# Last block of a small transformer: experts multiplied densely from streamed tables, in place of gathered rows

## What is computed

```python
q = einsum('cd,de->ce', xc, w_q).reshape(C, 8, 2, 128)
s = einsum('chpk,pnk->chpn', q, sub_keys)            # 8 heads, 2 halves, 128 keys each
sv, si = top_k(s, 16)
cand = sv[:, :, 0, :, None] + sv[:, :, 1, None, :]   # 16 x 16 sums
top_v, top_pos = top_k(cand, 16)
eid = take_along_axis(cand_id, top_pos)              # si0 * 128 + si1: one of 16384 experts
gate = softmax(top_v)
act = gelu(einsum('cd,chkd->chk', xc, expert_u[eid]))
y = einsum('chk,chkd->cd', gate * act, expert_v[eid])
```

## Time and profile before

| | us |
|---|---|
| runs before | 1394.95, 1395.61, 1398.93 (median 1395.61) |
| span of the profiled execution | 1393.4 |
| TensorE busy | 1274.3 (91%) |
| VectorE busy | 813.1 (58%) |
| ScalarE busy | 436.1 (31%) |
| POOL busy | 653.1 (47%) |
| bytes moved by DMA | 406.77 MB |

### The profile page before, as it was taken

The page is one execution under the profiler, slowest core; times in us unless marked ns, Lnnn a source line. Parts: engine busy times, 40 slices in busy tenths (PEclk is TensorE's granted clock), DMA queues, the critical chain, the costliest instruction groups (busy, mean ns, idle before and its releaser), DMA issues.

```text
span 1393.4 us, 17185 instructions
## 1 busy us (share of the span) xinstructions
PE 1274.3 (91%) x6328; PEld 785.6 (56%) x6328; DVE 813.1 (58%) x1694; ACT 436.1 (31%) x1065; POOL 653.1 (47%) x647
## 2 busy tenths in 40 slices
PE   9999999999999999999999999989677887877886
PEld 8887686648886686549655565633232333323332
DVE  1776377441666387352357764879888654444445
ACT  1533344111334334212334433243323232222223
POOL 0556667431636667422104444455533645554540
PEclk9999999999999999999999999999998989998999
DMA  9544335546444344635449999999999999999995
GB/s 374 213 167 173 131 125 209 210 157 222 152 170 179 122 167 170 254 137 208 172 171 412 420 406 421 419 419 421 422 421 421 421 423 421 422 421 422 422 421 240
DMA packets 54061, 406.77 MB, mean 292 GB/s; under 512 B 6213, under 2 KB 8666, under 8 KB 11610
## 3 DMA queue, kind: packets, MB, share of 16 engines
q0 software_dynamic: 37184, 268.45, 46.5%
q1 hardware_dynamic: 15706, 136.18, 25.3%
q10 hardware_dynamic: 1088, 1.05, 0.3%
HBM read 403.53 MB, written 1.07 MB: 290 GB/s over the span
## 4 chain that ended last, share of the span: by engine, by line
PE 33%; DMA 24%; DVE 6%; ACT 3%; issue 1%; POOL 0%; DVEq 0%; ACTq 0%
DMA ring<-in_peer_uv,vM 12%; PE bank L1173 11%; PE pj L739 6%; PE pj L775 6%; DMA qM<-in_peer_uv,vM 5%; DMA xT<-in_peer_uv,vM 4%; PE pj L1036 3%; PE pj L754 3%; DMA more_rows<-in_peer_uv,vM 2%; DMA b<-in_peer_uv,vM 2%; DVE ring L1993 1%; ACT rope L1409 1%; PE bank L699 1%; DVE qM L1993 0%; PE bank L1046 0%
## 5 line engine op out<-in xcount | busy, mean ns | idle before, releaser
L739 PE MATMUL pj<-xT,ring 128*128 128x256 f32 (+1 forms) x1568 | 318.4, 363 | 0.9 <-ACT hv L1343 0.4
L739 PEld LDWEIGHTS pj<-xT,ring 128*128 128x128 f32 x1568 | 276.6, 190 | 36.5 <-issue 2.6
L674 POOL DMA_INDIRECT ring<-in_peer_uv,vM x108 | 129.8, 1202 | 124.1 <-PE bank L1173 108.2
L635 POOL TENSOR_SCALAR more_rows<-more_rows,lbt 128x256 f32<-128x256 f32 x168 | 175.7, 1046 | 16.4
L1993 DVE SCALAR_TENSOR_TENSOR ring<-ring,memT 128x1024 f32<-128x1024 f32 x110 | 133.6, 1224 | 83.9 <-DMA ring<-in_peer_uv,vM 83.2
L1407 ACT ACTIVATE rope<-vM 128x1 f32<-128x1 f32 (+2 forms) x112 | 22.6, 202 | 385.1 <-DVE ring L1993 166.1
L1173 PE MATMUL bank<-ring,causal 128*128 128x512 f32 x256 | 123.5, 629 | 20.2 <-ACT causal L1415 20.2
L775 PE MATMUL pj<-ring,yT 128*128 128x512 f32 x320 | 140.8, 594 | 0.0
L633 POOL TENSOR_SCALAR mod_part<-more_rows,lbt 128x256 f32<-128x256 f32 x24 | 22.8, 951 | 245.7 <-issue 121.3
L636 POOL TENSOR_TENSOR mod_part<-mod_part,more_rows 128x256 f32<-128x256 f32 x168 | 128.4, 765 | 14.0
L1173 PE MATMUL bank<-ring,tri 128*128 128x512 f32 x176 | 84.8, 624 | 18.5 <-ACT tri L1415 18.4
(11 more groups left out here) (386 smaller groups left out, 2053.0 us busy)
## 6 DMA issues: line engine op xcount, KB each, us to landing
ring<-in_units SPq DMA_DIRECT2D x43, 2048.0 KB, 9.5
more_rows<-in_w_ada SPq DMA_DIRECT2D x24, 1024.0 KB, 4.9
ring<-in_units SPq DMA_DIRECT2D x2, 1536.0 KB, 8.0
ring<-in_peer_uv,vM POOLq DMA_INDIRECT x108, 21.4
memT<-in_mem SPq DMA_DIRECT2D x2, 512.0 KB, 5.3
ring<-in_units SPq DMA_DIRECT2D x1, 1024.0 KB, 8.9
xT<-in_x_turned SPq DMA_DIRECT2D x1, 1024.0 KB, 10.8
x<-in_x SPq DMA_DIRECT2D x1, 1024.0 KB, 16.3
```

The lines of the kernel that those rows point to most:

```text
L635: do(g.tensor_scalar(mod_w[:, c, :], mod_w[:, c, :], silu_c[:, c:c + 1], None, ALU.mult))
L674: pool.indirect_dma_start(row_slot[k], None, d["peer_uv_2"], bass.IndirectOffsetOnAxis(ap=expert[:, t, j:j + 1], axis=0))\
L739: ins = nc.tensor.matmul(pj[s][0:n, 2 * m + first:2 * m + stop], ring[:, slot, at:at + n], act[:, c, first:stop], start=(c == 0), stop=(c ...
```

## The change

The gather and all that hangs on it goes: the indirect DMAs, dots, diagonals, H, the parts of the routing, the 15 slots. In its place:

- The host lays the u table out in 32 units of 4 keys, channels on partitions, and the v table as it is (partition = first key, 128 x 1024 floats along it). After the last weight unit SP streams 32 u units and 32 v units of 2 MB through the same ring of three.
- Task A (64 of them, `pair_products`): two second keys k, all 128 first keys, all 256 tokens; 16 products of 128x256 with xT into a PSUM half. ScalarE's `pair_acts` takes gelu of it into `act_all`, 128 keys x 256 tokens of floats per partition, which lies over tiles that are dead by then.
- The routing is done per tile. `chosen` gives the two key numbers of each pick as floats; with the gate they are turned by TensorE (J, three transposes a tile) so that picks lie on partitions.
- For each batch of 8 tokens VectorE compares the key numbers with 0..127 (`hot_rows`, two operations of 1024 columns), POOL multiplies the second by the gate, and TensorE multiplies the two one-hot matrices for each token (B, 8 products of 128x128): a 128 x 128 table of gates. VectorE multiplies it into `act_all` (`batch_weights`).
- A0 to A31 come before the first batch, then A and B alternate. For keys that a batch comes before, ScalarE copies the gates into `act_all` (`batch_kept`) and POOL multiplies the late activations in (`late`).
- Task V (32 units, `value_sums`): for each of 128 second keys, the weights of a tile times 1024 columns of v, four products of 128x512 summed over all keys in four PSUM halves.
- Queries are made per tile and unit (K0t ... K3u, 32 products of 128x128 each), scores per unit and tile; row_gate2 and final_g are loaded late; the tiles' addresses are set by hand; the scratch for software DMA is set to 1024.

```diff
-            for n in range(ROWS):
-                t, j = n // PICKS, n % PICKS
-                k, previous, _ = PICK[n]
...
-                    pool.indirect_dma_start(row_slot[k], None, d["peer_uv_2"],
-                                            bass.IndirectOffsetOnAxis(ap=expert[:, t, j:j + 1], axis=0))\
-                        .then_inc(sem(f"row_load{k}"), 16)
...
+            for n in range(2 * EXPERT_UNITS):
+                r = FIRST_EXPERT + n
+                ring_released(sp, r)
+                src = (d["peer_u_2"][n] if n < EXPERT_UNITS else
+                       d["peer_v_2"][:, (n - EXPERT_UNITS) * DC * COLS:(n - EXPERT_UNITS + 1) * DC * COLS])
+                load(ring[:, r % RING, :], src, f"ring_load{r % RING}")
+                if n == EXPERT_UNITS + RING:
+                    gate_row(row_gate2, 5, "late_rows_load")
+                    load(final_g, d["final_g_2"].rearrange("(o n) -> o n", o=1).to_broadcast([P, D_MODEL]), "late_rows_load")
...
+            def gated(i):
+
+                pool.wait_ge(sem("hot_made"), 2 * (i + 1))
+                seconds = hot[:, i % 2, 1, :, :]
+                do(g.tensor_tensor(seconds, seconds, picks_turned[:, 2, i * BATCH:(i + 1) * BATCH].unsqueeze(2)
+                                   .to_broadcast([P, BATCH, NKEYS]), ALU.mult), "hot_ready")
+
+            def late(k):
+
+                n, tokens = k - FIRST_BATCH - 1, before_pair(k)
+                pool.wait_ge(sem("late_filled"), n + 1)
+                weights = act_all[:, 2 * k:2 * k + 2, 0:tokens]
+                do(g.tensor_tensor(weights, weights, late_acts[n % 2][:, :, 0:tokens], ALU.mult), "late_done")
...
+            def pair_products(task):
+
+                k, n = int(task[1:]), HALF[task]
+                slot = ring_loaded(pe, FIRST_EXPERT + k // 2)
+                half_empty(pe, n)
+                for i in range(2):
+                    for c in range(DC):
+                        at = (2 * (k % 2) + i) * D_MODEL + c * P
+                        ins = nc.tensor.matmul(half_bank[n % 4][:, i * T:(i + 1) * T], ring[:, slot, at:at + P], xT[:, c, :],
+                                               start=(c == 0), stop=(c == DC - 1))
+                last(ins, "half_filled")
+
+            def batch_gates(i):
+
+                pe.wait_ge(sem("hot_ready"), i + 1)
+                for q in range(2):
+                    key = (l, ("B", i, q))
+                    bank_empty(pe, key)
+                    for n in range(4):
+                        ins = nc.tensor.matmul(bank_of(key)[:, n * P:(n + 1) * P], hot[:, i % 2, 0, 4 * q + n, :],
+                                               hot[:, i % 2, 1, 4 * q + n, :], start=True, stop=True)
+                    last(ins)
+
+            def value_sums(n, tiles, halves=range(2)):
+
+                slot = ring_loaded(pe, FIRST_EXPERT + EXPERT_UNITS + n)
+                for at in range(4):
+                    k = 4 * n + at
+                    if k // 2 > FIRST_BATCH:
+                        pe.wait_ge(sem("late_done"), k // 2 - FIRST_BATCH)
+                    for t in tiles:
+                        for half in halves:
...
+                            ins = nc.tensor.matmul(half_bank[2 * t + half], act_all[:, k, t * P:(t + 1) * P],
+                                                   ring[:, slot, at * D_MODEL + half * COLS:at * D_MODEL + (half + 1) * COLS],
+                                                   start=(k == 0), stop=(k == NKEYS - 1))
...
+            def pair_acts(task):
...
+                if late:
+                    m = k - FIRST_BATCH - 1
+                    if m >= 2:
+                        act.wait_ge(sem("late_done"), m - 1)
+                    do(a.activation(late_acts[m % 2][:, :, 0:late], src[:, :, 0:late], ACT.Gelu), "late_filled")
+                do(a.activation(act_all[:, 2 * k:2 * k + 2, late:], src[:, :, late:], ACT.Gelu), f"half_free{n % 4}")
...
+            def hot_rows(i):
+
+                if i >= 2:
+                    bank_filled(dve, (l, ("B", i - 2, 1)))
+                dve.wait_ge(sem("picks_turned"), i * BATCH // P + 1)
+                for k in range(2):
+                    v.tensor_tensor(hot[:, i % 2, k, :, :], iota[:, :].unsqueeze(1).to_broadcast([P, BATCH, NKEYS]),
+                                    picks_turned[:, k, i * BATCH:(i + 1) * BATCH].unsqueeze(2).to_broadcast([P, BATCH, NKEYS]),
+                                    ALU.is_equal).then_inc(sem("hot_made"), 1)
+
+            def batch_weights(i):
+
+                first = before_batch(i)
+                dve.wait_ge(sem("acts_kept"), first // 2)
+                for q in range(2):
...
+                    t0 = i * BATCH + 4 * q
+                    weights = act_all[:, 0:first, t0:t0 + 4]
+                    v.tensor_tensor(weights, bank_of(key)[:, :].rearrange("p (t n) -> p n t", t=4)[:, 0:first, :], weights,
+                                    ALU.mult).then_inc(sem(bank_free(key)[0]), 1)
```

More of the change, by code:

```diff
@@ L68 @@
             """Xt BUt BKt Xu MT BUu BKu BQa BQb SK S0 S1 BVa S2 PL0 PL1 BVb P0 P1 S3 S4 Y0 S5 Y1 O1t P2 O0t P3 O1v Zt Y2 P4
[L69 to L72, removed]
+            K0t Y3 E0t P5 Y4 Y5 O1w O0v O0w K1t K2t E1t Zu K3t E2t K0u E3t K1u E0u K2u E1u K3u E2u A0 E3u A1 A2 A3 A4 A5
+            A6 A7 A8 A9 A10 A11 A12 A13 J0 A14 A15 A16 A17 A18 A19 A20 A21 A22 A23 A24 A25 A26 A27 A28 A29 J1 A30 A31
+            AB V0t V1t V2t V0u V1u V2u VV V29t V30t V31t V29ua V30ua V31ua V29ub V30ub V31ub"""]
 ACT_HEAD = ["MK", "X MK"]
@@ L76 @@
     Le18 HO2 HN2 HO3 HN3 LN"""
[L77 to L80, removed]
+ACT_LAST = """Xu BU BK BQa BQb SK S0 S1 MT S2 BV P0 P1 S3 S4 P2 S5 OMta OMtb P3 Zt P4 K0t E0t P5 OMua OMub K1t K2t E1t
+    Zu K3t E2t K0u E3t K1u E0u K2u E1u K3u E2u A0 E3u A1 A2 A3 A4 A5 A6 A7 A8 A9 A10 T0 A11 A12 A13 J0 A14 A15 A16 A17
+    A18 A19 A20 A21 A22 A23 A24 A25 A26 T1 A27 A28 A29 J1 A30 A31 AB FN0 FN1"""
 DVE_ORDER = """F0 N FP0 R0 R1 R2 R3 Da01 KR Da02 S0 Db01 P0 Db02 L01 S1 Da03 L02 AD Db03 Da04 F1 AD S2 Da05 L03 Da06
@@ L96, in pe_tasks @@
         tasks = []
-        for task in text.split():
+        for task in stage_tasks(text) if text == PE_ORDER[-1] else text.split():
             if task == "LD":
@@ L197, in bank_uses @@
         return [("MT",)]
-    if task[0] == "E":
+    if task[0] in "EJ":
         return [(task,)]
+    if task[0] == "B" and task[1:].isdigit():
+        return [("B", int(task[1:]), q) for q in range(2)]
     if l == B2 and task[0] == "Y":
@@ L241, in bank_index @@
         for task in TASKS[l]:
-            few = few or (l == B2 and task == "Zt")
+            few = (few or task == "Zt") and l == B2 and task != "O1w"
             if l == B2 and task == "Y2":
@@ L258, in bank_index, with before_pair, before_batch @@
     return out, uses
-def picks_order():
-    free, out, last = [], [], {}
-    for n in range(ROWS):
[L265 to L276, removed]
+HALF = {task: n for n, task in enumerate(
+    [t for t in TASKS[B2] if t[0] == "K"] + [t for t in TASKS[B2] if t[0] == "A" and t[1:].isdigit()])}
+ASIDE = [UNIT[B2, "K1"], UNIT[B2, "K2"]]
+RING_UNITS = [n for n in range(len(STREAM)) if n not in ASIDE]
+RING_AT = {n: r for r, n in enumerate(RING_UNITS)}
+FIRST_EXPERT = len(RING_UNITS)
+def before_pair(k):
+    return min(max(k - FIRST_BATCH, 0), BATCHES) * BATCH
+def before_batch(i):
+    return 2 * min(FIRST_BATCH + i + 1, PAIRS)
 def constants():
@@ L419, in build @@
[L419 to L426, removed]
-        spare_rows = [flat(more_rows), flat(kM)]
@@ L1029, in expert_queries @@
                     w = [ring[:, slot, c * COLS:(c + 1) * COLS] for c in range(DC)]
-                s, use = BIG[l, name]
-                first, stop = tiles[0] * P, tiles[-1] * P + P
-                pe.wait_ge(sem(f"pj_free{s}"), use)
-                after(pe, "xT_ready", l - 1, 2 * tiles[-1] + 5)
-                for m in columns:
-                    for c in range(DC):
-                        ins = nc.tensor.matmul(pj[s][:, 2 * m * P + first:2 * m * P + stop], w[c][:, m * P:(m + 1) * P],
-                                               xT[:, c, first:stop], start=(c == 0), stop=(c == DC - 1))
@@ L1038, in expert_queries @@
-                return ins
-            def sub_key_scores(key, ready, products):
+                n = HALF[task]
+                half_empty(pe, n)
+                after(pe, "xT_ready", l - 1, 2 * t + 5)
+                for m in range(4):
+                    for c in range(DC):
+                        ins = nc.tensor.matmul(half_bank[n % 4][:, m * P:(m + 1) * P], w[c][:, m * P:(m + 1) * P],
+                                               xT[:, c, t * P:(t + 1) * P], start=(c == 0), stop=(c == DC - 1))
@@ L1985, in dots_of @@
[L1985 to L1995 removed]
+                for k in range(2):
+                    do(v.tensor_copy(places[k], digits[k]), behind=1)
```

586 lines of the change are left out of this document (228 added, 358 removed).

## The result

| | before | after |
|---|---|---|
| median | 1395.66 us (4 runs, 1394.95 to 1398.93) | 1746.87 us (4 runs, 1746.41 to 1748.13) |
| span of the profiled execution | 1393.4 us | 1744.5 us |
| ratio | | 1.2513, 95% interval 1.2496 to 1.2531 |

The change makes the kernel 25% slower.

What follows compares the result with a forecast made beforehand. The gather stage was taken as DMA-bound, with TensorE not far behind. TensorE's new path to 1737.8 us, plus a 7.5 us tail, 4.3 idle and 2.2 around the span, gave 1752 us, range 1740 to 1790.

Steps and rivals of the forecast that it cites:

- What TensorE pays and what comes: TensorE's new products at 216, 429 and 112 ns per instruction: pair products 442.2 us, value sums 439.7, gates 57.2, transposes 0.8.
- V replaces the old sum one for one: Value sums on TensorE: 1024 instructions, 439.7 us, in place of the 512 products on gathered rows.
- the change gives nothing back here: Value sums on TensorE: their 439.7 us is just what the old products on gathered rows cost.
- rival 2: Long dense run on TensorE: lower clock, 10.7% more time, 100 us on 939, giving 1852 us; chance 2%.
- U and the gates: Pair products with the u table and gate-table products: 499 us on top of TensorE, which had some 112 us to spare.
- The path: TensorE's order of work: query scores start at 730.2 us, first pair products at 797.0, value sums end at 1737.8.
- the idle share of 4.3 us: TensorE's idle time over the new products: 0.46% of 941 us, taken from the 200 to 600 us stretch.
- The 2.2 us for what lies around the span: Outside the profiled span: 2.2 us added, the old kernel's median of 1395.61 over its span of 1393.4.
- What was costed at nothing: Ring loads, gelu, gate copies, routing and late weights: taken as hidden under TensorE's products, at no cost.
- hand-overs J0 and J1: Turning each tile's picks on TensorE: exponentials ready in time, first tile with 17 us margin, second turned at 1006 us.
- The alternating half: Pair products alternating with gate batches: TensorE's step 8.7 us, VectorE 3.8 to 5.2, POOL 3.6 to 6.3, all hidden.
- Rival 1: Alternating pair products and gate batches: bound by VectorE and POOL; a 10 us step gives 1792 us, 12 gives 1854; chance 7%.

Runs made afterwards that it cites:

- X1: Kernel after the change, with the gate products of every second token left out (4 of 8 per batch): 1718.99 us.
- x5: Kernel after the change, with the u-table pair products over the first 512 of 1024 channels only, tables still streamed whole: 1525.75 us.
- x2_pool_4: Kernel after the change, with POOL squaring the second one-hot table in place four more times for each batch: 1856.99 us.
- x7_uv_f32r_b: Kernel after the change, with u and v products on rounded float32r operands and shortened hand-overs: 1246.06 us, 0.8925 of the kernel before.
- x3_apart: Kernel after the change, without alternation: all u-table pair products first, then all 32 gate batches: 1826.62 us.

## Why the prediction was right, step by step

- *What TensorE pays and what comes.* The three rates held: V took 1736.94 - 1297.31 = 439.6 us (forecast 439.7); A0 to V 500.8 (501.1). X1 and x5 price the instructions apart, at 109 and 216 ns (112 and 216).
- *"V replaces the old sum one for one", and "the change gives nothing back here".* In instructions it does; in time the second part was wrong. The old sum was 482.81 + 3.60 busy us, the new one 439.6: 47 us less. Most of that is the clock: up to 900 us, at 1.00, a gathered instruction took 446 ns (99.85 us for 224), from there on, at 0.92, 484 ns (382.96 for 792), and in V 429. The prediction had the 10.7% in rival 2 and didn't use it here. Its sum was not hurt, since it adds up TensorE's path and not differences. The matmuls on gathered rows alone, by window:

```profile
740.00:900.00 160.00, 99.85 (x224) 41.38 (x224) 1.00 1.01 418
900.00:1394.00 494.00, 382.96 (x792) 158.30 (x792) 0.92 0.98 408
```

  U and the gates (499 us) less those 47 are 452 of the 454 us by which TensorE's busy time rose; the idle time that went (103 us) leaves the loss of 351. The forecast had 356.
- *The path.* A0 began at 796.56 (797.0); the output products at 729.89 (730.2). The tail was 1744.5 - 1736.9 = 7.6 us (7.5).
- *The one term of the sum that was clearly mis-sized* is the idle share of 4.3 us, taken from 200 to 600 us. The window from 740 us to the last matmul shows 0.06 us lost in 997:

```profile
740.00:1737.00 997.00, 996.94 (x4104) 698.45 (x4102) 236.24 (x580) 85.09 (x200) 84.23 (x63) 1.00 0.36 137
```

  Without the term the sum is 1747.5, and 1746.87 was measured. The 2.2 us for what lies around the span were 1.9 in the run that was profiled (1746.41 - 1744.5).
- *What was costed at nothing.* Ring loads land in 7.6 and 7.4 us, under the 13.8:

```profile
ring<-in_peer_u SPq DMA_DIRECT2D x32, 2048.0 KB, 7.6
ring<-in_peer_v SPq DMA_DIRECT2D x32, 2048.0 KB, 7.4
```

  Both hand-overs J0 and J1 were on time: VectorE stood waiting for the exponentials, 112.9 us in two waits, and TensorE had none. X5 halves the cover of the u stream and cuts that of the batch chain from 8.7 to 5.2 us, and still shows no wait. The strided gate copies took 0.37 us for 248 columns, under the 0.63 that was taken as their lower bound.
- *The alternating half.* POOL's product was 1.92 us, below the lower bound of 2.35; x2_pool_4 has both kinds side by side, 2.31 us with two full operands and 1.92 with a broadcast one, so broadcasting made it cheaper, not dearer (the squaring reads one tile twice, but the product of two tiles of the earlier trace rows took 2.35 too). The weightings were 0.43 us for 264 columns to 0.69 for 512: the nearest row was right, and the 16-byte pieces added nothing to it. Rival 1 needed 8.7 us and had 3.2 at most on POOL and 4.7 on VectorE.

The reason ahead of all this was the place to look: the gather stage was bound by DMA, so halving its bytes seemed the gain, but what the dense form buys them with is 499 us of the engine that was 79% busy beside it.

## What to carry to other kernels

A stage that is bound by one resource gives back only what the next one has to spare: here 7 + 105 us of TensorE, and some 47 us more on the old sum, mostly by the higher clock. Before a gather is traded for dense products, count the products at the price of their type in the trace (here two instructions of 216 or 429 ns each), since the same trade loses 25% at that price and wins 11% at one instruction each (in x7_uv_f32r_b, with fewer bits in the factors and against a kernel before that kept them all). And put a cover to the test by lengthening what lies under it: one more POOL operation cost nothing, four cost 110 us.

## What the runs showed of the hardware

**The port that VectorE and POOL share.** In the later batches of the kernel after, two comparisons take 3.31 us where they overlap POOL's product, and 2.35 where they don't:

```profile
1028.89 2.35 DVE L1920 TENSOR_TENSOR hot<-iota,vM 128x1024 f32<-128x1024 f32 x2
...
1262.86 1.90 POOL L679 TENSOR_TENSOR hot<-hot,vM 128x1024 f32<-128x1024 f32 x1
1263.08 0.66 DVE L1935 TENSOR_TENSOR act_all<-bank,act_all 128x480 f32<-128x480 f32 x1 [0.19 <-ACT act_all L1420]
1263.65 3.31 DVE L1920 TENSOR_TENSOR hot<-iota,vM 128x1024 f32<-128x1024 f32 x2
```

POOL's product ends at 1264.76, 1.11 us after the comparisons were issued, and they are 0.96 us longer. In x3_apart the two comparisons at 1303.67 us take 3.14 us beside a product that ends 0.93 us after their start, and the two at 1300.20, with no product beside them, 2.35. The delay is nearly the whole time that the product still had to run, so this is waiting and not sharing. The weighting beside it, with one operand from PSUM, took its usual 0.66. It agrees with the rule of the Trainium skill ("SBUF — State Buffer", section "SBUF: two separate sides") that the prediction weighed, for an operation with two operands in SBUF. Here 8.7 us of TensorE hide it; in x3_apart, where they don't, it is part of the 4.26 us a batch.

**Rounded operands.** A product of 128x512 took some 245 ns (16 in 3.9 us), in place of 859 (two instructions of 429.4), and rounding 2048 columns 1.90 us on ScalarE and 1.23 on VectorE. Not tried: whether fewer bits are fit for another use of this layer, and a form of the routing that would let U begin earlier.
